# Another order of the group norm between the scan and the output projection, its low parts on GpSimd, and alternating PSUM banks at the end of the state space model

## The chip, the cores and the metric

The kernel runs on one core of one Trainium2 chip. The metric is the device time of one execution in microseconds, as the median over several executions. The profiled execution of the kernel before took 3902.99 us, of which its span (first to last instruction) is 3901.2 us.

## The reference, cut to what matters

The network works on 1024 positions of 1024 features, all in float32, and has three layers. The first layer is a gated linear recurrence, the second an RWKV-7 time mix, each followed by a feed-forward part, and the third a hybrid of a long convolution and a state space model. Two places of it matter here.

The end of the RWKV time mix is a group norm over each head of 64 features, a bias, a bonus term, a gate and the output projection:

```python
mean = jnp.mean(y, axis=-1, keepdims=True)
var = jnp.mean(jnp.square(y - mean), axis=-1, keepdims=True)
yn = ((y - mean) * lax.rsqrt(var + RW_GN_EPS)).reshape(B, T, D)
yn = yn * ln_w + ln_b
out = (yn + bonus) * g
return out @ w_o, v_first
```

The state space model of the third layer computes, for each of 32 groups of 16 channels, a complex linear recurrence of 64 states and reads it out; a GELU follows. Beside it stands the layer norm of the convolution's result:

```python
_, _, s_re, s_im = lax.associative_scan(combine, (a_re, a_im, bu_re, bu_im), axis=1)
y = (einsum("blgp,ghp->blgh", s_re, c_re) - einsum("blgp,ghp->blgh", s_im, c_im) + d * uf)
y = gelu(y)
cu = silu(layer_norm(cu, conv_ln_g, conv_ln_b))
```

## The kernel before, in words

Features lie on the 128 partitions in eight tiles (`DT` = 8) of 1024 positions each. Every engine has its own instruction list, written out by hand in the order in which it is issued; semaphores (`after(name, n)`, `tick(name)`) join the lists. An engine that meets a wait stands still with all that is behind it. PSUM is used as four banks of 128 x 1024 float32, which the profile calls psA to psD (`ps[0]` to `ps[3]`). Blocks end with a barrier between the engines.

**Projections.** A large matrix product is made of strips of weights (class `Flow`). Each operand is split into a high part (rounded to `float32r` by a ScalarE copy, `hi`, line 259) and a low part (the rest, one subtraction; for weights on GpSimd, `lo`, line 269), and three products are added: high x high, high x low, low x high. One tile k of one strip is six matmuls of 512 columns (`product`, line 302).

**The group norm, `TimeMixOut` (lines 3036 to 3232).** For each of the eight tiles k of `o` (rw_o in the profile): TensorE sums over the heads (`head_sum` in `sums`, line 3087), VectorE subtracts the mean (`centre`, line 3186), ScalarE squares (`square`, line 3124), TensorE sums the squares (`head_sum` in `spreads`), ScalarE takes Ln and then Exp with a scale of -0.5 (`roots`, lines 3131 and 3135), VectorE applies the root, the bias with the bonus and the gate in three instructions (`gated`, lines 3192, 3196 and 3199), ScalarE makes the high part (`high`, line 3139) and VectorE the low part (`low`, line 3203). Then TensorE multiplies tile k with the first two strips `at[0]` and `at[1]` of the output projection. When all eight tiles are through, it does the six strips `at[2:]` whole. SyncE loads the bonus tile (`load`) and brings one tile of H back (`back`) behind `gated`; `fast.load` then fetches the weights of the feed-forward part.

The order before goes in pairs q = 0 to 3. TensorE: sums 0 and 1, spreads 0, sums 2, spreads 1, sums 3, and then for each pair the products of its two tiles, with spreads 2 behind the products of pair 0 and spreads 3 behind those of pair 1. VectorE: six `centre`, then for each pair two `gated` and two `low`, with the last two `centre` behind pair 0. ScalarE: high parts of a pair, then the roots of the pair after the next. The banks of spreads 2 (psC, psD) are those of sums 3, so they need the last two `centre`; the buffers of the roots go round by four. GpSimd has only the low parts of weights in this stretch.

**The end of the state space model, `ssm` (lines 3775 to 4044).** The 32 groups go in four parts k (`SU` = 4). VectorE makes the states of part k (`group`, about a dozen instructions). TensorE's `outputs(k)` (lines 3861 and 3863) makes for each of eight groups one matmul of the direct part and two of the states, all into psD; VectorE copies the two halves of psD out (`outputs` on VectorE, line 3997); TensorE's `back(k)` turns them over into psA (line 3870), and ScalarE's GELU reads psA (line 3950). TensorE's `outputs(k)` waits until psD has been copied out (`sy_c` at 2k), and `back(k)` until the GELU before has read psA (`sy_t` at k). Between them lies the variance of the layer norm (`variance`, line 3885, psB), whose root ScalarE makes with Ln and Exp (lines 3946, 3948); VectorE's `normed` (line 4009) applies it to the eight tiles of H, four before its `outputs(2)` and four before its `outputs(3)`. At the barrier behind it the block of the next projections begins (first weights `w_glu`, line 248).

## Time and profile before

| | |
|---|---|
| median of 3 runs | 3901.69 us (3901.31 to 3909.06) |
| the profiled execution | 3902.99 us |
| its span | 3901.2 us |
| mean granted TensorE clock | 0.965 |
| busy: PE, PEld, DVE, ACT, POOL | 92%, 74%, 66%, 39%, 30% of the span |
| group norm with the first two strips | about 2027.9 to 2110.9 us of the span |
| state space model | about 3488.7 to 3602.4 us of the span |

In the rows PE is TensorE's matmuls, PEld its weight loads, DVE is VectorE, ACT ScalarE, POOL GpSimd and SP SyncE. A row of the timeline gives the start in us, the length in us, the engine, the line and operation, what it writes and reads with its shape, how often it stands there (xN, merged), and in brackets the idle time of the engine before it and what ended it.

### The profile page before, as it was taken

The page shows a single profiled execution, that of the slowest core. Times are in us where ns is not written, and L with a number is a line of the kernel's source. Part 1 is how long each engine was busy: PE and PEld are TensorE (multiplying, and loading weights), DVE is VectorE, ACT ScalarE, POOL GpSimd, SP SyncE. Part 2 cuts the span into 40 slices and gives each one's busy share as a digit, 9 for nine tenths or more (in the row PEclk, how much of TensorE's full clock was granted, in tenths as well). Part 3 has the DMA queues.
Part 4 walks back from the last instruction along what each step waited for, and adds up shares of the span by engine and source line. Part 5 has one row for each costly group of instructions (what it writes and reads, how often), then busy time and mean ns, then how long its engine had stood idle before and what let it go on. Part 6 is the DMA issues. An engine that isn't in the chain of part 4 may idle for free. (4 is left out here: it accounts for less than half of the span.)

```text
span 3901.2 us, 57647 instructions
## 1 busy us (share of the span) xinstructions
PE 3577.1 (92%) x24956; PEld 2905.9 (74%) x24956; DVE 2570.5 (66%) x2287; ACT 1536.5 (39%) x1634; POOL 1152.7 (30%) x521
## 2 busy tenths in 40 slices
PE   8999999999989998877777999999998999997997
PEld 6778788878767776666655788878886888875775
DVE  5554767687756857766655666678758888816532
ACT  5563432344534338744444433343443222113312
POOL 1125454555421211233322445445520000000211
PEclk9999999999999999999998999999999999997998
DMA  2112233344212245712113123253312222231322
GB/s 97 49 38 62 70 108 104 104 158 171 68 55 82 107 144 163 237 63 73 69 46 113 46 98 111 92 185 131 115 48 106 75 75 78 82 141 30 144 95 103
DMA packets 187037, 383.74 MB, mean 98 GB/s; under 512 B 16080, under 2 KB 84816, under 8 KB 181008
## 3 DMA queue, kind: packets, MB, share of 16 engines
q1 hardware_dynamic: 149216, 307.68, 23.8%
q10 hardware_dynamic: 37568, 72.36, 5.0%
q8 instruction: 198, 3.24, 0.3%
q14 instruction: 55, 0.45, 0.0%
HBM read 273.57 MB, written 105.91 MB: 97 GB/s over the span
## 5 line engine op out<-in xcount | busy, mean ns | idle before, releaser
L3817 POOL MEMSET ssm_toep<- 128x4096 f32 x1 | 3.5, 3512 | 545.7 <-POOLq L3516 545.7
L3403 DVE SCALAR_TENSOR_TENSOR H<-hy_cu,par,H 128x1024 f32<-128x1024 f32 x120 | 153.5, 1279 | 0.0
L269 POOL TENSOR_TENSOR wlo1C<-fast_raw,whi1C 128x1024 fp32r<-128x1024 f32 (+1 forms) x40 | 110.9, 2773 | 113.4 <-ACT whi1C L259 113.4
L269 POOL TENSOR_TENSOR wlo0B<-fast_raw,whi0B 128x1024 fp32r<-128x1024 f32 (+1 forms) x40 | 112.1, 2802 | 107.5 <-ACT whi0B L259 107.5
L3403 DVE SCALAR_TENSOR_TENSOR hy_odd<-hy_cu,par,hy_odd 128x1024 f32<-128x1024 f32 x112 | 143.3, 1280 | 0.0
L269 POOL TENSOR_TENSOR wlo1A<-fast_raw,whi1A 128x1024 fp32r<-128x1024 f32 (+1 forms) x40 | 111.4, 2785 | 105.6 <-ACT whi1A L259 105.6
L269 POOL TENSOR_TENSOR wlo1B<-fast_raw,whi1B 128x1024 fp32r<-128x1024 f32 (+1 forms) x39 | 107.9, 2766 | 114.3 <-ACT whi1B L259 114.3
L1007 DVE TENSOR_TENSOR fast_xl<-fast_xr,fast_xh 128x2048 fp32r<-128x2048 f32 (+1 forms) x42 | 127.5, 3059 | 21.3 <-ACT fast_xh L848 21.3
L269 POOL TENSOR_TENSOR wlo0A<-fast_raw,whi0A 128x1024 fp32r<-128x1024 f32 (+1 forms) x40 | 110.1, 2753 | 105.0 <-ACT whi0A L259 105.0
L269 POOL TENSOR_TENSOR wlo0C<-fast_raw,whi0C 128x1024 fp32r<-128x1024 f32 (+1 forms) x39 | 108.0, 2770 | 104.2 <-ACT whi0C L259 104.2
L942 DVE TENSOR_TENSOR fast_g<-fast_g,flow_rms 128x1024 f32<-128x1024 f32 x44 | 127.0, 2886 | 1.5
L2942 DVE STREAM_TRANSPOSE sc_XX<-sc_XX 64x512 f32<-64x512 f32 x160 | 112.9, 706 | 17.3 <-POOL sc_XX L2882 12.4
L2889 POOL TENSOR_TENSOR sc_NT<-sc_Gx,sc_level 128x512 f32<-128x512 f32 x80 | 100.1, 1282 | 78.1 <-PE psB L2627 43.4
L834 ACT ACTIVATE fast_g<-fast_g 128x1024 f32<-128x1024 f32 x44 | 46.6, 1060 | 127.4 <-DVE fast_g L942 127.4
L2627 PE MATMUL psA<-sc_XX,sc_NT 64*64 64x64 f32 x1280 | 55.7, 234 | 40.9 <-issue 40.8
L269 POOL TENSOR_TENSOR wlo0A<-wraw0A,whi0A 128x1024 fp32r<-128x1024 f32 (+2 forms) x15 | 33.8, 2256 | 195.5 <-ACT whi0A L259 195.5
L269 POOL TENSOR_TENSOR wlo0C<-wraw0A,whi0C 128x1024 fp32r<-128x1024 f32 (+1 forms) x16 | 37.6, 2347 | 172.7 <-ACT whi0C L259 172.7
L2627 PEld LDWEIGHTS psA<-sc_XX,sc_NT 64*64 64x64 f32 x1280 | 48.6, 143 | 47.1 <-issue 45.8
L2627 PE MATMUL psB<-sc_XX,sc_NT 64*64 64x64 f32 x1280 | 51.7, 235 | 31.6 <-issue 29.9
L848 ACT ACTIVATE fast_xh<-fast_xr 128x2048 fp32r<-128x2048 f32 (+1 forms) x42 | 74.1, 1765 | 12.1 <-DMA fast_xr<-ffn_x 11.8
L2363 DVE SCALAR_TENSOR_TENSOR flow_rms<-flow_rms,hawk_room_b 128x1024 f32<-128x1024 f32 x10 | 12.3, 1225 | 101.0 <-ACT flow_rms L2202 101.0
L959 DVE TENSOR_TENSOR fast_g<-fast_g,fast_s 128x1024 f32<-128x1024 f32 x22 | 72.7, 3303 | 0.8
(1458 smaller groups left out, 11925.8 us busy)
## 6 DMA issues: line engine op xcount, KB each, us to landing
fast_raw<-ffn_in_dram SPq DMA_DIRECT2D x88, 512.0 KB, 3.8
fast_xr<-ffn_x SPq DMA_DIRECT2D x28, 1024.0 KB, 6.1
sc_ops<-rw_arbkv SPq DMA_DIRECT2D x15, 1280.0 KB, 7.2
fast_raw<-ffn_out_dram SPq DMA_DIRECT2D x32, 512.0 KB, 3.8
wraw1A<-hybrid_in_dram SPq DMA_DIRECT2D x24, 512.0 KB, 3.4
wraw1B<-hybrid_in_dram SPq DMA_DIRECT2D x24, 512.0 KB, 3.3
ffn_x<-fast_g ACTq DMA_DIRECT2D x22, 512.0 KB, 3.3
ffn_x<-fast_e ACTq DMA_DIRECT2D x22, 512.0 KB, 2.8
```

The source lines that it names most:

```text
L269: eng.tensor_tensor(self.slot(wlo, n), self.raw[n], self.slot(whi, n).bitcast(fp32), ALU.subtract)\
L834: act.activation(g[:, :, z, :], g[:, :, z, :], ACT.Silu).then_inc(*tick("q_silu"))
L848: act.activation(part(hx, v, i), part(lr, v, i), ACT.Copy).then_inc(*tick("x7_hi"))
L942: dve.tensor_tensor(g[:, :, h, :], g[:, :, h, :], wide(h), ALU.mult).then_inc(*tick("q_g"))
L959: dve.tensor_tensor(g[:, :, 1, :], g[:, :, 1, :], s[:, :, :], ALU.mult).then_inc(*tick("q_h"))
L1007: dve.tensor_tensor(part(lx, v, i), part(lr, v, i), part(hx, v, i).bitcast(fp32), ALU.subtract)\
L2363: dve.scalar_tensor_tensor(out=e, in0=e, scalar=1.0, in1=tz, op0=ALU.add, op1=ALU.mult)\
L2627: mm = pe.matmul(eight[2 * a][half(e), m, :], NT[half(1 - e), a, (5 * (n // 2) + l) % 3, m, :], XX[half(1 - e), n % 4, 1, m, :], start=Tru ...
L2889: pl.tensor_tensor(NT[:, n % 2, k % 3, :, :], Gx[:, n % 2, :, :], by_m(slevel[:, l, :]), ALU.mult)\
L2942: dve.transpose(XX[half(1 - e), n % 4, 1, :, :].rearrange("p m t -> p (m t)"), XX[half(e), n % 4, 0, :, :].rearrange("p m t -> p (m t)")). ...
L3403: op = dve.scalar_tensor_tensor(out=acc, in0=c[:, j:j + T], scalar=w, in1=acc, op0=ALU.mult, op1=ALU.add)
L3817: pl.memset(toep[:, :, :], 0.0).then_inc(*tick("st_zero"))
```

## The change

It has two parts, which touch different stages.

In the group norm, TensorE's spreads 2 (tiles 4 and 5) now stand behind sums 3, ahead of every product, and spreads 3 behind the products of tile 1. VectorE does `gated(0)`, then the last two `centre`, then `gated(1)` to `gated(7)`; it has no `low` any more. The eight `low` stand on GpSimd, six of them ahead of the weight strip 2 (`W.lo(pl, 2)`) and two behind it. ScalarE's high parts are spread one by one between squares and roots, and the high part of the weight strip 2 stands ahead of the last two.

In the state space model, parts k write psD and psC in turn (`ps[3 - k % 2]`), so that `outputs(k)` waits for the copy of part k - 2 (part 1 for `sb_b`, the last reader of psC). TensorE's `outputs(3)` is cut in two halves of four groups with `back(2)` between them, and `back(3)` goes to psB (`ps[k // (SU - 1)]`), which it may once the Ln has read the variance (`ln_log`). VectorE does its `outputs(2)` before any `normed`, then six of them, `outputs(3)`, and the last two.

```diff
                     sums(2)
                     spreads(1)
                     sums(3)
-                    for q in range(DT // 2):
-                        if q == 0:
-                            W.begin(pe, at[0])
-                            W.begin(pe, at[1])
-                        for k in (2 * q, 2 * q + 1):
-                            pe.wait_ge(*after("ro_lo", k + 1))
-                            W.product(pe, at[0], k, *self.xs[k])
-                            W.product(pe, at[1], k, *self.xs[k])
-                        if q < 2:
-                            spreads(q + 2)
+                    spreads(2)
+                    W.begin(pe, at[0])
+                    W.begin(pe, at[1])
+                    for k in range(DT):
+                        pe.wait_ge(*after("ro_lo", k + 1))
+                        W.product(pe, at[0], k, *self.xs[k])
+                        W.product(pe, at[1], k, *self.xs[k])
+                        if k == 1:
+                            spreads(3)
...
                     squares(1)
                     roots(0)
                     squares(2)
+                    high(0)
                     roots(1)
-                    for q in range(DT // 2):
-                        high(2 * q)
-                        high(2 * q + 1)
-                        if q == 0:
-                            squares(3)
-                        if q + 2 < DT // 2:
-                            roots(q + 2)
+                    high(1)
+                    squares(3)
+                    high(2)
+                    roots(2)
+                    high(3)
+                    roots(3)
+                    high(4)
+                    high(5)
                     W.hi(act, 2)
+                    high(6)
+                    high(7)
...
                 @block.gpsimd
                 def _(pl):
+                    def low(k):
+                        pl.wait_ge(*after("ro_hi", k + 1))
+                        pl.tensor_tensor(self.lo[:, k, :], o[:, k, :], self.hi[:, k, :].bitcast(fp32), ALU.subtract).then_inc(*tick("ro_lo"))
+
+                    W.lo(pl, 1)
+                    for k in range(6):
+                        low(k)
+                    W.lo(pl, 2)
+                    for k in range(6, DT):
+                        low(k)
...
-                    for q in range(DT // 2):
-                        gated(2 * q)
-                        gated(2 * q + 1)
-                        low(2 * q)
-                        low(2 * q + 1)
-                        if q == 0:
-                            centre(DT - 2)
-                            centre(DT - 1)
+                    gated(0)
+                    centre(DT - 2)
+                    centre(DT - 1)
+                    for k in range(1, DT):
+                        gated(k)
...
-                        def outputs(k):
+                        def outputs(k, groups=range(8)):
...
+                            elif k == 1:
+                                pe.wait_ge(*after("sb_b", SU))
                             else:
-                                pe.wait_ge(*after("sy_c", 2 * k))
-                            for g in range(8):
+                                pe.wait_ge(*after("sy_c", 2 * k - 2))
+                            for g in groups:
                                 q, rows = g // 2, slice(64 * (g % 2), 64 * (g % 2) + 64)
-                                to = ps[3][:, g % 2, q * P:(q + 1) * P]
+                                to = ps[3 - k % 2][:, g % 2, q * P:(q + 1) * P]
...
                         def back(k):
                             pe.wait_ge(*after("sy_c", 2 * k + 2))
-                            pe.wait_ge(*after("su_c", SU) if k == 0 else after("sy_t", k))
+                            if k == 0:
+                                pe.wait_ge(*after("su_c", SU))
+                            elif k < SU - 1:
+                                pe.wait_ge(*after("sy_t", k))
+                            else:
+                                pe.wait_ge(*after("ln_log", 1))
...
-                        for k in range(SU + 1):
-                            if k < SU:
-                                outputs(k)
-                            if k > 0:
-                                back(k - 1)
-                            if k == 0:
-                                variance(0)
-                                variance(1)
-                            if k == 1:
-                                for m in range(2, DT):
-                                    variance(m)
+                        outputs(0)
+                        variance(0)
+                        variance(1)
+                        outputs(1)
+                        back(0)
+                        for m in range(2, DT):
+                            variance(m)
+                        outputs(2)
+                        back(1)
+                        outputs(3, range(4))
+                        back(2)
+                        outputs(3, range(4, 8))
+                        back(3)
...
                         group(3)
-                        for k in range(4):
-                            normed(k)
                         outputs(2)
-                        for k in range(4, DT):
+                        for k in range(6):
                             normed(k)
                         outputs(3)
+                        for k in range(6, DT):
+                            normed(k)
```

## Rows read from the trace of the kernel before

**Rows 1.** The page, busy time, share of the span and instructions of each engine.

```profile
PE 3577.1 (92%) x24956; PEld 2905.9 (74%) x24956; DVE 2570.5 (66%) x2287; ACT 1536.5 (39%) x1634; POOL 1152.7 (30%) x521
```

**Rows 2.** Windows: stretch, length, busy us (instructions) by engine, granted clock, DMA.

```profile
2027.90:2110.90 83.00, 56.57 (x160) 34.09 (x161) 50.26 (x43) 48.24 (x46) 7.17 (x3) 0.84 0.41 143
2110.90:2198.00 87.10, 86.65 (x379) 70.78 (x378) 48.49 (x38) 43.10 (x48) 41.63 (x22) 1.00 0.12 39
3488.70:3602.40 113.70, 93.27 (x480) 64.41 (x480) 76.18 (x90) 31.79 (x26) 3.51 (x1) 0.83 0.29 87
```

**Rows 3.** Timeline of TensorE in the group norm.

```profile
2047.38 1.88 PE L3087 MATMUL psD<-rw_o,const 128*128 128x512 f32 x4
2057.32 1.19 PE L302 MATMUL psA<-ro_oh,whi1A 128*128 128x512 f32 x2 [8.06 <-DVE ro_ol L3203]
2061.71 0.62 PE L302 MATMUL psA<-ro_oh,whi1A 128*128 128x512 f32 x2
...
2095.47 1.22 PE L302 MATMUL psA<-ro_oh,whi1A 128*128 128x512 f32 x2 [6.72 <-DVE ro_ol L3203]
2105.29 0.74 PE L302 MATMUL psA<-ro_oh,whi1A 128*128 128x512 f32 x2 [1.20 <-DVE ro_ol L3203]
2110.91 0.62 PE L302 MATMUL psC<-ro_oh,whi1C 128*128 128x512 f32 x2
```

**Rows 4.** Timeline of VectorE in the group norm.

```profile
2045.42 1.28 DVE L3192 SCALAR_TENSOR_TENSOR rw_o<-rw_o,par,flow_rms 128x1024 f32<-128x1024 f32 x1 [2.29 <-ACT flow_rms L3135]
...
2104.02 2.43 DVE L3203 TENSOR_TENSOR ro_ol<-rw_o,ro_oh 128x1024 fp32r<-128x1024 f32 x2
```

**Rows 5.** Timeline of ScalarE in the group norm: roots and high parts.

```profile
2050.55 1.11 ACT L3131 ACTIVATE ro_rs<-psB,eps 128x1024 f32<-128x1024 f32 x1
2051.68 1.28 ACT L3135 ACT_TABLE_LOAD   x1
2052.97 2.00 ACT L3135 ACTIVATE ro_rs<-ro_rs 128x1024 f32<-128x1024 f32 x2
2054.88 1.99 ACT L3139 ACTIVATE ro_oh<-rw_o 128x1024 fp32r<-128x1024 f32 x2
```

**Rows 6.** Timeline of GpSimd and VectorE, three places where both have work.

```profile
2034.94 2.37 POOL L269 TENSOR_TENSOR wlo1A<-wraw1A,whi1A 128x1024 fp32r<-128x1024 f32 x1 [48.85 <-ACT whi1A L259]
2035.04 1.23 DVE L3186 SCALAR_TENSOR_TENSOR rw_o<-psD,rw_o 128x1024 f32<-128x1024 f32 x1 [0.49 <-PE psD L3087]
...
2419.31 3.46 POOL L269 TENSOR_TENSOR wlo1B<-fast_raw,whi1B 128x1024 fp32r<-128x1024 f32 x1 [3.40 <-ACT whi1B L259]
...
3630.26 2.41 POOL L269 TENSOR_TENSOR wlo2B<-wraw2A,whi2B 128x1024 fp32r<-128x1024 f32 x1 [3.21 <-ACT whi2B L259]
3630.34 3.42 DVE L3711 TENSOR_TENSOR hb_cl<-H,hb_ch 128x1024 fp32r<-128x1024 f32 x1
```

**Rows 7.** Timeline of TensorE at the end of the state space model.

```profile
3575.45 1.09 PE L3870 MATMUL psA<-const,ssm_u 128*128 128x128 f32 x8
3579.45 0.64 PE L3861 MATMUL psD<-ssm_toep,ssm_ut 128*128 128x128 f32 x2 [2.91 <-DVE ssm_u L3997]
...
3594.29 1.97 PE L3870 MATMUL psA<-const,ssm_u 128*128 128x128 f32 x8
3598.44 1.94 PE L3870 MATMUL psA<-const,ssm_u 128*128 128x128 f32 x8 [2.18 <-ACT ssm_y L3950]
```

**Rows 8.** Timeline of VectorE and ScalarE there.

```profile
3573.24 4.87 DVE L4009 SCALAR_TENSOR_TENSOR H<-H,par,hb_rs 128x1024 f32<-128x1024 f32 x4 [3.37 <-ACT hb_rs L3948]
3578.03 1.28 DVE L3997 COPY ssm_u<-psD 128x512 f32<-128x512 f32 x2
...
3600.42 2.00 ACT L3950 ACTIVATE ssm_y<-psA 128x1024 f32<-128x1024 f32 x1 [2.12 <-PE psA L3870]
```

**Rows 9.** Windows at the end of the state space model.

```profile
3547.50:3556.80 9.30, 9.30 (x58) 7.35 (x57) 8.93 (x12) 1.06 (x1) 0.00 (x0) 1.00 0.00 0
3584.00:3590.00 6.00, 6.00 (x21) 4.66 (x22) 0.09 (x1) 0.00 (x0) 0.00 (x0) 0.50 0.00 0
```

More of the change, by code:

```diff
@@ L3199, in gated @@
                         dve.tensor_tensor(x, x, gates_kept[k], ALU.mult).then_inc(*tick("ro_gated"))
-                    def low(k):
-                        dve.wait_ge(*after("ro_hi", k + 1))
-                        dve.tensor_tensor(self.lo[:, k, :], o[:, k, :], self.hi[:, k, :].bitcast(fp32), ALU.subtract).then_inc(*tick("ro_lo"))
                     for k in range(6):
                         centre(k)
-                    for q in range(DT // 2):
-                        gated(2 * q)
-                        gated(2 * q + 1)
-                        low(2 * q)
-                        low(2 * q + 1)
-                        if q == 0:
-                            centre(DT - 2)
-                            centre(DT - 1)
+                    gated(0)
[3 more added lines that the diff above has]
+                        gated(k)
                     for m, n in enumerate(at):
@@ L3863, in outputs @@
                                     mm = pe.matmul(to, ee[rows, k, z, q, 0:SN], cq[rows, k, z, q, SSM_H:], start=False, stop=(z == 1))
-                            mm.then_inc(*tick("pe_yc"))
+                            if groups[-1] == 7:
+                                mm.then_inc(*tick("pe_yc"))
                         def back(k):
                             pe.wait_ge(*after("sy_c", 2 * k + 2))
-                            pe.wait_ge(*after("su_c", SU) if k == 0 else after("sy_t", k))
+                            if k == 0:
[4 more added lines that the diff above has]
+                                pe.wait_ge(*after("ln_log", 1))
                             for i in range(SC):
-                                mm = pe.transpose(ps[0][:, i // 4, (i % 4) * P:(i % 4 + 1) * P],
+                                mm = pe.transpose(ps[k // (SU - 1)][:, i // 4, (i % 4) * P:(i % 4 + 1) * P],
                                                   yc[:, k, i, :, :].rearrange("p g h -> p (g h)"), ident)
@@ L3949, in _ @@
                             act.wait_ge(*after("pe_yt", k + 1))
-                            act.activation(y[:, k, :].rearrange("p (c i) -> p i c", i=SC), flat[0].rearrange("p (i c) -> p i c", i=SC),
+                            act.activation(y[:, k, :].rearrange("p (c i) -> p i c", i=SC), flat[k // (SU - 1)].rearrange("p (i c) -> p i c", i=SC),
                                            ACT.Gelu_apprx_tanh).then_inc(*tick("sy_t"))
@@ L3997, in outputs @@
                                 dve.tensor_copy(yc[:, k, :, e:8:2, :].rearrange("p i q h -> p q i h"),
-                                                ps[3][:, e, :].rearrange("p (q i h) -> p q i h", q=4, i=SC)).then_inc(*tick("sy_c"))
+                                                ps[3 - k % 2][:, e, :].rearrange("p (q i h) -> p q i h", q=4, i=SC)).then_inc(*tick("sy_c"))
                         ch(dve.memset(ee[:, :, :, :, 0:1], 0.0))
```

## The prediction

> **What bounds the kernel now.** The busy shares of the profile's page come first: PE is busy 92% of the span, so time is to be had only where TensorE stands or runs at the low clock [rows 1]. The windows over the two changed stages show both: in the group norm TensorE is busy 56.6 of 83.0 us at a mean granted clock of 0.84, in the state space model 93.3 of 113.7 us at 0.83, while in the 87 us behind the group norm it is busy all but 0.5 us at 1.00 [rows 2]. So whatever the group norm finishes earlier is handed on: the strips behind it are TensorE's own work, back to back. No other engine is the bound of either stage as a whole (VectorE 50 and ScalarE 48 of 83 us), so each is a chain of hand-overs.
>
> In the group norm the reader sees TensorE end the spreads at 2049.26 (2047.38 + 1.88), stand 8.06 us for a low part, later 6.72 and 1.20 us (a like gap of 10.15 lies between), and begin strip 2 without a gap at 2110.91 [rows 3]. Behind each long gap the first pair of strips takes 4.4 us (2057.32 to 2061.71), where at full clock it takes 2.73. The chain through those gaps is spreads, roots, two `gated`, two high parts, two low parts, products, and only then the next spreads. VectorE ends `gated(7)` at 2104.02, where the last two low parts begin [rows 4].
>
> In the state space model `outputs(3)` starts 2.91 us after `back(1)`, because it waits for the copy of psD, and then takes from 3579.45 to 3594.29, 14.8 us [rows 7], at clock 0.50 [rows 9]. `outputs(1)` and `back(0)` together took 9.3 us at 1.00 [rows 9]. `back(2)` stands behind it, and `back(3)` waits 2.18 us for the GELU of part 2; the last GELU ends at 3602.42 [rows 8], and the next block starts there.
>
> **Part A, the group norm.** Nothing changes until `gated(0)` starts at 2045.42. The steps used below: one `gated` is three instructions of 1.28, 1.28 and 1.22, with hand-over 3.8 us [rows 4]; the same lengths stand in all eight. A pair's roots are a table load 1.28, two Ln 2.1, a table load 1.28, two Exp 2.0, together 6.6 us; a high part is 1.0 [rows 5]. A low part leaves VectorE, where a pair costs 2.43 [rows 4], and costs GpSimd 2.4 each, by the like subtraction for weights [rows 6].
>
> What decides the sum is whether the two engines work side by side. At 3630.26 GpSimd starts such a subtraction of 2.41 us, and VectorE's, begun 0.08 us later, lasts 3.42 in place of 1.22: it stood until 3632.67. At 2419.31 it is GpSimd's that lasts 3.46. But VectorE's `centre` at 2035.04, which reads PSUM and one SBUF tile, takes 1.23 beside GpSimd's 2.37 [rows 6]. All three instructions of `gated` read two SBUF tiles, so I count them as excluded by each low part, and `centre` as free. The Trainium skill, "SBUF — State Buffer", section Who interferes with whom, has this as a rule: a VectorE instruction with two SBUF inputs and a GpSimd instruction that reads SBUF block each other fully, and the one issued first wins. It speaks against the move of the low parts, and by it the sum comes out as mine and not as the second rival's.
>
> The schedule: `gated(0)` ends at 2049.3, the last two `centre` at 2051.2. Spreads 2 run from about 2050 to 2053.7, not from 2064. ScalarE makes high 0 at 2049.3 to 2050, roots 1 until 2056.5, high 1, squares 3, high 2 until 2063, roots 2 until 2069.6, high 3, roots 3 until 2077, and high 4 and 5 by 2079.3. VectorE from 2051.2 has seven `gated`, 7 x 3.8 = 26.5 us, interrupted by eight GpSimd instructions (low 0 to 5, weight strip 2, low 6); the first costs 1.1, the others about 2.2 each, 16.7 us in all. It waits hardly at all in between (about 1 us for roots 4, partly paid by an interruption already counted). So `gated(7)` ends at 2051.2 + 26.5 + 16.7 = 2094.4, against 2104.0. High 7 ends at 2095.5 and low 7 at 2098.0. The product of tile 6 has been done by 2096.5; that of tile 7 is 2.7 us at full clock and 5.1 at the low one. TensorE has stood 1.5 us before it and 3 to 5 us before tile 6, so I take 4.4 to 4.9, and strip 2 begins at 2102.4 to 2102.9. Its weights are split by 2087.4. That is 8.5 to 8.0 us before 2110.91; I take 8.0.
>
> What is moved past what: SyncE's bonus loads and H transfers wait for `gated` in the same order, with at least 7.6 us from each load's start to its use; the feed-forward weights start with `gated(7)`, 8 us before strip 2 instead of 6.9. Squares 3 and high 0 to 2 cost ScalarE nothing on the path, since VectorE is the later one. The added waits are GpSimd's for high parts: behind low 6 and 7 stands only later weight work, and in front of strip 2's low part low 5, which cannot hold TensorE before the last product. TensorE's early spreads 2 put products 0 and 1 behind 3.6 us that it would else have idled.
>
> Bounds of A: if nothing excludes, `gated(7)` waits for roots 3 only and ends near 2081, GpSimd ends its row of low parts at 2087.4, and the last products end at 2094.6: 16.3 us gained. If each of the eight interruptions costs VectorE a whole further turn (3.3 in place of 2.2, as a third party at each switch), 8.8 more are lost and A is worth about -0.5 to 0. I take 8.0, from the measured 3.42.
>
> **Part B, the state space model.** Up to `back(1)` (3575.45 to 3576.4) TensorE keeps its order without gaps, and `outputs(1)` could start no sooner before. Then `outputs(3)`, first half, starts at 3576.5: psC was copied out long before, and the states of part 3 are ready. At full clock a whole `outputs` is 9.3 - 0.95 = 8.4 us [rows 7, 9], a half 4.2: to 3580.7. VectorE now copies part 2 at 3575.5 to 3576.8, ahead of `normed`, and the GELU of part 1 ends at 3578.6 as before, so `back(2)` runs without a wait, to 3581.7. Second half to 3585.9. Six `normed` of 1.2 [rows 8] end at 3584.0, so VectorE copies at 3585.9 to 3587.2; `back(3)` needs only the Ln, to 3588.3; the last GELU, 2.0, ends at 3590.3, and the last two `normed` at 3589.6. Against 3602.42 that is 12.1 us; I take 12.0. What hid the four `normed` was GELU and copy; six of them have 9 us of matmuls over them.
>
> Of the 12 us, 6.5 are the clock: 14.8 - 8.4. It fell while TensorE stood for 2.91 us, and that gap is gone. But 15 us of unbroken `outputs` did not bring it back, so this kind of work is near the point where the clock isn't kept, and now 18.8 us of it stand in a row. The lower bound: the clock falls at 3579.5 all the same. Then the first half ends at 3581.6, `back(2)` at 3583.5, the second half, 7.4, at 3590.9, copy, `back(3)` and GELU (1.3 + 1.9 + 2.0) at 3596.3: 6.1 gained. Low from 3576.5 on: 3.7. No bound lies above 12.5.
>
> The Trainium skill, "TensorE: Matmul & The Clock Gate", section What's actually happening, says that sustained activity releases the throttle. Rows 9 don't agree for this work: busy all of the time, and 0.50. By that rule of the Trainium skill B would be 12.0 whatever the gap; by the row it hangs on never losing the clock.
>
> **Sum.** 3902.99 - 8.0 - 12.0 = 3883.0 for an execution like the profiled one. The median of the runs is 1.3 lower, so 3881.7.
>
> **The rivals.** *The clock falls in B anyway*: for it, no `outputs` run longer than 9.3 us at 1.00 is in the trace and none at 0.50 recovers; against it, the clock held through three such runs and fell only after a gap. 3.7 to 6.1 in place of 12.0: 3887.6 to 3890.0. The Trainium skill, "TensorE: Matmul & The Clock Gate", section Part 4: PE-mode transpose, says that transposes don't count as activity for the clock; by it `back(1)` and `back(2)` inside the long run would make this rival likelier.
>
> *GpSimd and VectorE don't exclude each other here*: for it, only two-input subtractions and additions are seen blocked in rows 6, not `gated` itself; against it, these differ in nothing that should matter. A is 16.3: 3873.4.
>
> *Exclusion at a full turn each*: A is worth nothing, 3889.7. Speaking for it is only that so many hand-overs in a row stand nowhere in the trace.
>
> *Only one part arrives*, because a transfer or the block behind fills its place: for B, the next block's first matmul waits for weights loaded after the barrier, which move with it; for A rows 2 show no slack. If neither arrived, 3901.7.
>
> *Slower*: the products of tiles 6 and 7 start at the low clock after a chain of short stands, and the clock stays low in the strips behind, as it stayed in `outputs(3)`. A strip is 10.9 us at full clock and 20.5 at the low one (0.857 against 0.455 per pair of matmuls behind 2095.47), 9.6 lost for each. After two strips at the low clock the 20 us are gone, after three the kernel is slower, 3910. Against it: behind all three long gaps these matmuls had the full clock within 3.4 to 6.1 us.
>
> **How the numbers follow.** Forecast 0.66, with its own range 3877 to 3887; clock lost in B 0.12; no exclusion 0.08; full turns 0.06; one part or none arrives 0.05; slower 0.03. The range leaves out the no-exclusion case and what lies above 3891: 3876 to 3891. A measurement of this kernel tells about 0.2%, 7.8 us, from no change. Faster by more than that (below 3893.9) are the first four cases, 0.92, less a little for both small gains together: 0.91. Within it 0.06, slower 0.03.
>
> **What would show it.** A right: no `low` on VectorE, `gated` instructions of 3.4 us in about eight places, between the second `centre` pair and strip 2; strip 2 starts 75 us (2102.7 - 2027.9) into the stage in place of 83. Wrong if `gated` keeps 1.28 throughout. B right: `outputs(3)` begins directly behind `back(1)` at clock 1.00 and the stage is 101.7 us long in place of 113.7; wrong if the clock reads 0.50 before `back(3)`. The handing on is wrong if TensorE shows new gaps in the strips behind.

## The result, and the profile after

The changed kernel takes 3883.6 us (median of 6 runs, 3874.46 to 3891.65) against 3901.5 us (median of 6, 3899.82 to 3909.06). The ratio is 0.9949, 95% interval 0.9933 to 0.9965: 20 us faster by the ratio, 14 to 26 by its interval. The forecast was 3881.7 us, 20 us faster. The profiled execution took 3877.22 us, one of the two fastest, with a span of 3875.4 us, 25.8 shorter than that of the profiled execution before.

Windows over the two stages and the strips behind the group norm, the changed kernel; they answer to [rows 2]. Columns as there.

```profile
2028.60:2101.90 73.30, 58.07 (x160) 34.23 (x161) 56.58 (x35) 48.28 (x46) 29.07 (x11) 0.88 0.46 161
2101.90:2189.00 87.10, 86.65 (x379) 70.81 (x378) 48.32 (x38) 43.07 (x48) 41.65 (x22) 1.00 0.12 40
3476.20:3578.10 101.90, 85.17 (x480) 58.56 (x480) 76.19 (x90) 31.88 (x26) 3.43 (x1) 0.90 0.32 97
```

The group norm is 73.3 us long in place of 83.0, the state space model 101.9 in place of 113.7. The strips behind the group norm have the same 86.65 busy us in 87.10: what was gained was handed on. The 25.8 us of the span add up from the stretches between the same instructions of both traces: group norm -9.7, state space model -11.8, from strip 2 to the start of the state space model -3.6 (1377.8 to 1374.2), before the group norm +0.7, behind the state space model -1.4. The last three, 4.3 us, lie where nothing was edited. Most of the -3.6 arises at one place of the feed-forward part, about 520 us behind strip 2, where the kernel before stands 2.31 us and goes on at the low clock, while the changed kernel has neither there. TensorE of the kernel before there:

```profile
2633.99 0.66 PE L491 MATMUL psD<-fast_xh,whi1C 128*128 128x512 f32 x1 [2.31 <-DVE fast_xl L1007]
```

Whether this is an effect of the change stays open. The six traces with low parts on GpSimd (the changed kernel and five of those below) have 1373.4 to 1374.3 us in this stretch, the two with the old group norm 1377.9. But of three later kernels with one and the same third order of the group norm (low parts on VectorE, the high part of weight strip 2 early), two show 1377.7 and one 1374.6, so a difference of this size also comes without any edit.

Timeline of TensorE in the group norm, changed kernel, answering to [rows 3]:

```profile
2051.30 1.95 PE L3087 MATMUL psC<-ple_gate,const 128*128 128x512 f32 x4 [1.30 <-DVE rw_o L3199]
...
2061.98 1.22 PE L302 MATMUL psA<-ro_oh,whi1A 128*128 128x512 f32 x2 [4.21 <-POOL ro_ol L3179]
...
2093.21 1.22 PE L302 MATMUL psA<-ro_oh,whi1A 128*128 128x512 f32 x2 [4.07 <-POOL ro_ol L3179]
2099.08 0.73 PE L302 MATMUL psA<-ro_oh,whi1A 128*128 128x512 f32 x2 [0.38 <-POOL ro_ol L3179]
2101.92 0.62 PE L302 MATMUL psC<-ro_oh,whi1C 128*128 128x512 f32 x2
```

The reader sees spreads 2 at 2051.3, ahead of all products, and in place of stands of 8.06, 10.15 and 6.72 us three of 4.07 to 4.21 us (two are shown) and short ones. The releaser is now GpSimd's low part. The last product, from 2099.08 to 2101.92, had the full clock; the one of tile 6, from 2093.21 on, the low clock for all of its 5.5 us.

Timelines of VectorE and then of GpSimd, changed kernel, at the end of the group norm; they answer to [rows 4] and [rows 6]:

```profile
2078.41 1.22 DVE L3212 TENSOR_TENSOR rw_o<-rw_o,tm_g_last 128x1024 f32<-128x1024 f32 x1
2079.55 3.45 DVE L3205 SCALAR_TENSOR_TENSOR rw_o<-rw_o,par,ro_rs 128x1024 f32<-128x1024 f32 x1
2083.04 3.27 DVE L3209 SCALAR_TENSOR_TENSOR rw_o<-ro_bn,par,rw_o 128x1024 f32<-128x1024 f32 x1
2086.34 3.30 DVE L3212 TENSOR_TENSOR rw_o<-rw_o,tm_g_last 128x1024 f32<-128x1024 f32 x1
2089.57 1.27 DVE L3205 SCALAR_TENSOR_TENSOR rw_o<-rw_o,par,ro_rs 128x1024 f32<-128x1024 f32 x1
2090.88 3.36 DVE L3209 SCALAR_TENSOR_TENSOR rw_o<-ro_bn,par,rw_o 128x1024 f32<-128x1024 f32 x1
2094.27 1.23 DVE L3212 TENSOR_TENSOR rw_o<-rw_o,tm_g_last 128x1024 f32<-128x1024 f32 x1
```

```profile
2079.57 5.66 POOL L3179 TENSOR_TENSOR ro_ol<-rw_o,ro_oh 128x1024 fp32r<-128x1024 f32 x2 [4.80 <-ACT ro_oh L3138]
2085.19 3.38 POOL L269 TENSOR_TENSOR wlo1C<-wraw1A,whi1C 128x1024 fp32r<-128x1024 f32 x1
2090.81 2.34 POOL L3179 TENSOR_TENSOR ro_ol<-rw_o,ro_oh 128x1024 fp32r<-128x1024 f32 x1 [2.25 <-ACT ro_oh L3138]
2096.66 2.36 POOL L3179 TENSOR_TENSOR ro_ol<-rw_o,ro_oh 128x1024 fp32r<-128x1024 f32 x1 [3.51 <-ACT ro_oh L3138]
```

`gated(6)` takes three instructions of 3.3 to 3.45 us, since GpSimd has three subtractions to do at that time (low 4, low 5 and weight strip 2), and the two engines take turns. In the whole stage eight of VectorE's `gated` instructions are lengthened, as many as GpSimd has subtractions ahead of the end of `gated(7)`. Together they are 15.7 us longer than they would be alone.

TensorE, VectorE and ScalarE at the end of the state space model, changed kernel; the rows answer to [rows 7, 8]:

```profile
3562.48 1.09 PE L3884 MATMUL psA<-const,ssm_u 128*128 128x128 f32 x8
3563.41 0.39 PE L3869 MATMUL psC<-ssm_toep,ssm_ut 128*128 128x128 f32 x2
3563.73 0.71 PE L3871 MATMUL psC<-ssm_cq,ssm_e 64*128 64x128 f32 x4
...
3574.04 1.97 PE L3884 MATMUL psB<-const,ssm_u 128*128 128x128 f32 x8 [1.38 <-DVE ssm_u L4013]
```

```profile
3562.65 1.29 DVE L4013 COPY ssm_u<-psD 128x512 f32<-128x512 f32 x2 [5.75 <-PE psD L3871]
3563.86 7.25 DVE L4025 SCALAR_TENSOR_TENSOR H<-H,par,hb_rs 128x1024 f32<-128x1024 f32 x6
3572.70 1.29 DVE L4013 COPY ssm_u<-psC 128x512 f32<-128x512 f32 x2 [1.58 <-PE psC L3871]
```

```profile
3568.66 2.06 ACT L3966 ACTIVATE ssm_y<-psA 128x1024 f32<-128x1024 f32 x1 [3.00 <-PE psA L3884]
3576.05 2.00 ACT L3966 ACTIVATE ssm_y<-psB 128x1024 f32<-128x1024 f32 x1 [5.32 <-PE psB L3884]
```

`outputs(3)` begins directly behind `back(1)`, at 3563.41, and is over at 3572.65: 9.2 us with `back(2)` in it, where it took 14.8 alone. The windows over the row from `outputs(2)` to the end of `outputs(3)`, over `outputs(3)` with `back(2)` alone, and over `back(3)`, show the clock:

```profile
3554.10:3572.60 18.50, 18.50 (x113) 14.59 (x111) 11.16 (x12) 11.40 (x8) 0.00 (x0) 1.00 0.00 0
3563.40:3572.60 9.20, 9.20 (x58) 7.25 (x56) 7.71 (x7) 4.12 (x2) 0.00 (x0) 1.00 0.00 0
3574.00:3576.00 2.00, 1.96 (x8) 1.57 (x8) 2.00 (x2) 0.00 (x0) 0.00 (x0) 0.50 0.00 0
```

### The profile page after: what moved, and what is told of

It is laid out like the page before. It is cut to its first block and busy times, and to the rows that moved or that the text cites. A ratio compares the mean times of both kernels' runs of the same rounds, so it can differ in the third digit from the quotient of the medians.

```text
span 3875.4 us, 57648 instructions
## 1 busy us (share of the span) xinstructions
PE 3568.7 (92%) x24956; PEld 2898.7 (75%) x24956; DVE 2576.1 (66%) x2279; ACT 1536.1 (40%) x1634; POOL 1176.7 (30%) x529
## 5 line engine op out<-in xcount | busy, mean ns | idle before, releaser
L269 POOL TENSOR_TENSOR wlo0A<-fast_raw,whi0A 128x1024 fp32r<-128x1024 f32 (+1 forms) x40 | 110.1, 2752 | 105.1 <-ACT whi0A L259 105.1
L2882 POOL TENSOR_TENSOR sc_XX<-sc_XX,sc_eye 128x512 f32<-128x512 f32 x16 | 20.3, 1268 | 179.7 <-DVE sc_XX L2937 179.7
```

Source lines behind the costliest of these rows:

```text
L269: eng.tensor_tensor(self.slot(wlo, n), self.raw[n], self.slot(whi, n).bitcast(fp32), ALU.subtract)\
L2882: pl.tensor_tensor(XX[:, n % 4, 0, :, :], XX[:, n % 4, 0, :, :], by_m(seye[:, :]), ALU.add)\
```

## The experiments

The theory after the result: each part does by itself what its stage shows; GpSimd's low parts cost VectorE more than they take off it; the clock in the state space model is lost in a stand or just behind it, and `outputs` doesn't win it back. Rivals are named with each kernel. Stage lengths below are counted alike in each trace: the group norm from its first head sum to strip 2, the state space model from its first mean to the end of the last GELU. The ratios are to the kernel before on the same chip. The reader should weigh them with two facts: the times of one and the same code differ by 17 us between executions of the changed kernel and by up to 21 us in the kernels below, and each trace shows one execution.

**Each part alone.** The first kernel has the changed group norm only, the second the changed state space model only; their edits are those of the diff above.

> Part A alone: the group norm as changed, the state space model as before. My theory (the two parts are independent and what the group norm gains is handed on): strip 2 starts 9.7 us earlier than before, counted from the start of the stage (74.0 in place of 83.0 us or a little less), and the kernel is 8 to 10 us faster, ratio 0.9975 +- 0.0005. The rival (much of the 18 to 26 us comes from elsewhere, by chance between runs): under 5 us.

> Part B alone: the end of the state space model as changed, the group norm as before. My theory: the last GELU ends 11.4 us earlier against the start of the stage, clock 1.00 in all of outputs(3), and the kernel is 11 to 12 us faster, ratio 0.9970 +- 0.0005. The rival that the clock is lost in some executions of this stage: a few times stand 6 to 8 us above the others, and the gain is 4 to 8 us in those.

Norm alone: 3892.22 us (7 runs, 3887.63 to 3899.81), ratio 0.9971, interval 0.9960 to 0.9981; group norm 73.32 us, state space model 113.36. State space model alone: 3891.32 us (5 runs, 3889.37 to 3893.42), ratio 0.9966, interval 0.9952 to 0.9979; group norm 83.07, state space model 102.26. Both did in their stage what they do together, to within 0.4 us. By the ratios they are worth 11.3 and 13.3 us, so the rival of the first (under 5 us, the rest chance) fell. The sum is 24.6, against 20 for both; the intervals (the sum's reaches from 16 to 34) allow that they simply add. That the clock is lost in some executions of the second didn't show in its five times.

**Low parts on VectorE again.** The order of the changed kernel stays, the eight low parts move:

```diff
 # VectorE
                     gated(0)
                     centre(DT - 2)
                     centre(DT - 1)
-                    for k in range(1, DT):
+                    low(0)
+                    gated(1)
+                    for k in range(2, DT):
                         gated(k)
+                        low(k - 1)
+                    low(DT - 1)
 # GpSimd: without low
```

> As the changed kernel, but the eight low parts of the group norm are on VectorE again, each one gated part later (gated 2, low 1, gated 3, low 2 and so on). My theory (the two engines exclude each other, so each low part on GpSimd costs VectorE 2.2 us where it would itself need 1.2): gated(7) ends some 7 us earlier than in the changed kernel, strip 2 starts 6 to 9 us earlier, total 6 to 9 us faster than the changed kernel, ratio to before about 0.993. The rival (GpSimd takes the low parts off VectorE's hands and that is what gains): VectorE has 9.8 us more to do, strip 2 starts 3 to 9 us later than in the changed kernel.

3872.73 us (4 runs, 3870.55 to 3874.38), ratio 0.9918, interval 0.9905 to 0.9932. The group norm is 68.21 us long, 5.1 less than in the changed kernel. Timeline of VectorE in that kernel, `gated(6)` to the last low parts:

```profile
2078.30 1.28 DVE L3195 SCALAR_TENSOR_TENSOR rw_o<-rw_o,par,ro_rs 128x1024 f32<-128x1024 f32 x1
2079.62 3.29 DVE L3199 SCALAR_TENSOR_TENSOR rw_o<-ro_bn,par,rw_o 128x1024 f32<-128x1024 f32 x1
2082.95 1.23 DVE L3202 TENSOR_TENSOR rw_o<-rw_o,tm_g_last 128x1024 f32<-128x1024 f32 x1
2084.09 1.22 DVE L3206 TENSOR_TENSOR ro_ol<-rw_o,ro_oh 128x1024 fp32r<-128x1024 f32 x1
...
2089.00 2.43 DVE L3206 TENSOR_TENSOR ro_ol<-rw_o,ro_oh 128x1024 fp32r<-128x1024 f32 x2
```

Only one `gated` is still lengthened, 3.29 us, by the one GpSimd subtraction that is left there (weight strip 2). VectorE is through with `gated(7)` at about 2089.0, 60.7 us into the stage, against 66.9 in the changed kernel, although six low parts of its own, 7.3 us, stand ahead of that; the last two follow. The rival (GpSimd takes work off VectorE) has fallen: the new order alone gives 14.8 us, and the move to GpSimd takes 5.1 back, which leaves the 9.7 that the group norm gained. Which share the order of each of the three engines has in the 14.8, no run separates. The 5.1 are a little less than the 6 to 9 expected: `gated(7)` came 6.1 us earlier, but TensorE, whose product of tile 5 ran at the low clock (5.3 us), had those of tiles 6 and 7 still to do. The whole kernel became 12 us faster by the two ratios, more than the stage explains; their intervals only just don't touch.

**The weight's low part last.**

```diff
 # GpSimd
                     W.lo(pl, 1)
-                    for k in range(6):
-                        low(k)
-                    W.lo(pl, 2)
-                    for k in range(6, DT):
+                    for k in range(DT):
                         low(k)
```

> As the changed kernel, but GpSimd's low part of weight strip 2 stands behind all eight low parts of the group norm instead of between the sixth and the seventh. One interruption fewer ahead of gated(7): by my theory gated(7), the last low part and strip 2 come 2.0 to 2.3 us earlier, the weight's low part then ends about when the last product does. Rival (GpSimd's own row of low parts decides, not the exclusion): the same 2.2 us, but gated(7) on VectorE ends where it did.

3884.1 us (5 runs, 3878.52 to 3885.55), ratio 0.9945, interval 0.9932 to 0.9957, not to be told from the changed kernel. The group norm is 71.25 us long, 2.05 less, and `gated(7)` ends 2.06 us earlier in it, so the rival, by which it would end where it did, fell: one interruption of VectorE is worth what was said. The same trace brought something else: its state space model is 110.1 us long, 8 more, with the same code there. Windows over states(3), `outputs(0)`, the two variances and `outputs(1)` of that kernel:

```profile
3514.50:3518.00 3.50, 3.50 (x32) 3.23 (x32) 3.36 (x5) 0.00 (x0) 0.00 (x0) 0.50 0.00 0
3518.00:3533.00 15.00, 15.00 (x50) 11.40 (x48) 6.61 (x9) 1.02 (x1) 0.00 (x0) 0.50 0.01 1
3533.00:3538.70 5.70, 5.70 (x9) 2.42 (x9) 5.28 (x9) 1.06 (x1) 0.00 (x0) 0.61 0.00 0
3538.80:3547.00 8.20, 8.20 (x49) 6.37 (x47) 7.00 (x9) 1.06 (x1) 0.00 (x0) 1.00 0.00 0
```

TensorE is busy all of the time, yet the clock stays at 1.2 GHz through all 15 us of `outputs(0)` and rises only in the variances, whose matmuls have 512 columns. In the kernel before and in the changed one the clock had risen in the last 0.3 to 0.4 us of states(3) (mean 0.54 and 0.56), just before `outputs(0)`.

**Variances ahead of outputs(0).**

```diff
+                        variance(0)
+                        variance(1)
                         outputs(0)
-                        variance(0)
-                        variance(1)
                         outputs(1)
```

> As the changed kernel, but TensorE's variance of tiles 0 and 1 (wide matmuls, 512 columns) stands ahead of outputs(0) instead of behind it. One trace has shown outputs(0) at clock 0.50 from end to end where the matmuls before it did not raise the clock in time, and that stage 8 us longer. My theory (the clock of this stage is a lottery that outputs can't win back once lost, and it is behind most of the spread of the times): the two wide products raise the clock before outputs(0) in every execution, the stage is 99 to 101 us long, the spread of the times shrinks and the median falls 1 to 4 us under the changed kernel's. Rival (the spread comes from elsewhere, the scan above all): same median within 1 us and same spread.

3879.87 us (5 runs, 3870.86 to 3882.12), ratio 0.9938, interval 0.9925 to 0.9951. In the trace states(3) again ended at the low clock (3.68 us), the variances raised it, and the stage was 101.8 us long: in one execution the edit did what it was meant to. That it does so in each is not shown. The median fell by 3.7 us, as expected, but the two intervals overlap, and five times that still spread over 11 us, against six over 17, don't bear out that this stage makes most of the spread. The group norm of this trace, the same code as in the changed kernel, took 76.4 us against 73.3. Its first head sums ran at the low clock, which cost 1.7 us, and its last product stood 2.84 us and then took 4.45 us in place of 2.84. Window over that product:

```profile
2103.34:2107.79 4.45, 4.45 (x13) 3.49 (x13) 1.22 (x1) 1.43 (x2) 0.43 (x1) 0.62 1.03 371
```

**One bank.**

```diff
-                            elif k == 1:
-                                pe.wait_ge(*after("sb_b", SU))
                             else:
-                                pe.wait_ge(*after("sy_c", 2 * k - 2))
+                                pe.wait_ge(*after("sy_c", 2 * k))
...
-                                to = ps[3 - k % 2][:, g % 2, q * P:(q + 1) * P]
+                                to = ps[3][:, g % 2, q * P:(q + 1) * P]
... # and VectorE's copy reads ps[3] for every k
```

> As the changed kernel, but all four outputs(k) go to psD and wait for its copy as before; the earlier copy on VectorE, the split outputs(3) and back(3) in psB stay. My theory (what made the gap before outputs(3), and with it the low clock, was VectorE's four normed ahead of the copy, not the one bank): the gap is 0.4 to 0.5 us, the clock stays at 1.00, and the stage is only 0.5 us longer than in the changed kernel, 100.5 us. Rival (the alternating bank is what pays): outputs(3) starts 1.5 us or more late, the clock is lost, the stage is 106 us or longer.

3888.06 us (6 runs, 3869.81 to 3891.2), ratio 0.9955, interval 0.9939 to 0.9972. The stage is 111.0 us long in the trace, a length that the rival had named (106 or more), but not for the rival's reason: `outputs(0)` had the low clock from end to end, as above, which costs 8 us by itself. The place in question, TensorE of that kernel in front of `outputs(3)` and the window over it:

```profile
3574.56 0.46 PE L3867 MATMUL psD<-ssm_toep,ssm_ut 128*128 128x128 f32 x2 [0.51 <-DVE ssm_u L4011]
```

```profile
3574.60:3583.80 9.20, 9.20 (x56) 7.28 (x56) 6.98 (x6) 3.60 (x2) 0.00 (x0) 1.00 0.00 0
```

The stand is 0.51 us, the clock stays at 1.00, and from there to the end of the last GELU it is 14.7 us as in the changed kernel (14.6). Against the kernel with the same loss in `outputs(0)` (110.1) the stage is 0.9 longer. So it was VectorE's four `normed` ahead of the copy that made the stand of 2.91 us, and the alternating banks give about 0.5 to 0.9 us of the 11.8. Counted from the rows, the stand and the clock of `outputs(3)` are together 9.7 us, the second bank's share in it; about 1.8 lie behind `outputs(3)`, where its split and `back(3)` in psB act, which no run tests by themselves, and 0.4 ahead of `back(1)`, where the order of TensorE is unchanged.

**A stand put back.**

```diff
                         back(1)
+                        pe.wait_ge(*after("ln_n", 3))
                         outputs(3, range(4))
```

> As the changed kernel, with one wait more: TensorE waits for the third normed before outputs(3), which puts a gap of about 4 us there. My theory (the clock falls in the gap and outputs can't raise it again): outputs(3) runs at 0.50, and the stage is 4 + 6.5 = 10 to 11 us longer than in the changed kernel. Rival (the clock was lost for another reason, or comes back within outputs(3)): 4 to 6 us longer.

3893.24 us (12 runs, 3883.98 to 3899.74), ratio 0.9973, interval 0.9963 to 0.9983. The stage is 113.2 us long, 11.3 more than in the changed kernel. Timeline and windows of that kernel, the stand and `outputs(3)` with `back(2)` behind it:

```profile
3571.54 0.80 PE L3869 MATMUL psC<-ssm_toep,ssm_ut 128*128 128x128 f32 x2 [4.01 <-DVE H L4026]
```

```profile
3567.50:3571.50 4.00, 0.03 (x1) 0.00 (x0) 4.00 (x5) 2.04 (x1) 0.00 (x0) 0.86 0.00 0
3571.50:3588.20 16.70, 16.66 (x56) 13.00 (x56) 3.57 (x3) 2.01 (x1) 0.00 (x0) 0.50 0.00 0
```

4.0 us of stand, and 16.7 us in place of 9.2 behind it, all at 0.50. By the rival (the clock comes back within `outputs(3)`) it would have been 4 to 6 us in all. So this is the price of the clock in this stage shown by itself: 7.5 us on top of a stand of 4.0.

**Versions to beat both.** Three kernels have the low parts on VectorE and the high part of weight strip 2 ahead of `high(0)`:

```diff
                     squares(2)
+                    W.hi(act, 2)
                     high(0)
...
                     high(5)
-                    W.hi(act, 2)
                     high(6)
```

The first also rearranges the state space model: variances 0 to 5 in TensorE's idle time before states(3), `outputs(0)` before states(3), variances 6 and 7 behind `back(0)` and `back(1)`, the root behind the second GELU, ScalarE's squares 0 to 5 ahead of its own last work on the states, and four `normed` in place of six ahead of VectorE's last copy. The second moves variance 5 behind states(3). The third has the changed kernel's order with variances 0 and 1 ahead.

```diff
 # TensorE, first; the second has range(5), and variance(5) behind states(SU - 1)
-                        states(SU - 1)
+                        for m in range(6):
+                            variance(m)
                         pe.wait_ge(*after("ln_c", DT))
                         outputs(0)
-                        variance(0)
-                        variance(1)
+                        states(SU - 1)
                         outputs(1)
                         back(0)
-                        for m in range(2, DT):
-                            variance(m)
+                        variance(6)
                         outputs(2)
                         back(1)
+                        variance(7)
                         outputs(3, range(4))
```

> A version that may beat both. Group norm with the low parts on VectorE and the high part of weight strip 2 ahead of high(0), where ScalarE waits anyway, so that GpSimd's subtraction doesn't stand among the gated; state space model with variances 0 to 5 in TensorE's idle time before states(3), outputs(0) before states(3), variance 6 behind back(0), variance 7 behind back(1), the root behind the second GELU and four normed before the last copy. My theory: strip 2 starts 2 us earlier than with low parts on VectorE alone (66 us into the stage), and the state space model is 92 us long at best (VectorE's four groups end 1.3 us earlier, then outputs(3) at full clock), in all 8 to 11 us under the 3872.7 of that version: 3862 to 3865. Rival: a short gap before outputs(2) or outputs(3) loses the clock and 6 us of it.

> As the version with both stages rearranged, but variance 5 stands behind states(3), in the 1.78 us in which TensorE stood there and after which outputs(1) lost the clock. My theory (a short stand followed by outputs loses the clock; wide matmuls in it keep it): outputs(1) stays at 1.00, VectorE's copy comes 3 us earlier, the state space model takes 96 to 97 us in place of 99.5, median 2 to 4 us lower than that version's. Rival (each gap of 1 to 2 us that is left can lose the clock just as well): no gain, the loss moves to another outputs.

> The group norm of that version (low parts on VectorE, high part of weight strip 2 early) with the changed kernel's state space model, variances 0 and 1 ahead of outputs(0). My theory: group norm 65.5 us, state space model 101.8 us, so 2 to 3 us slower than the version with both stages rearranged and 6 to 8 us faster than the one that has only the variances ahead: about 3871 to 3874. Rival (the parts take from each other): above 3877.

First: 3870.54 us (4 runs, 3868.07 to 3874.45), ratio 0.9919 (0.9906 to 0.9932); group norm 65.5, state space model 99.5. Second: 3873.4 us (5 runs, 3865.87 to 3874.23), 0.9919 (0.9906 to 0.9931); 67.2 and 101.0. Third: 3870.4 us (5 runs, 3870.19 to 3875.6), 0.9919 (0.9906 to 0.9933); 65.5 and 102.3. The early high part did its 2 us and a bit in the stage (68.2 to 65.5); that it shows in the kernel's time can't be said. The 92 us hoped for in the state space model of the first and the 96 to 97 of the second didn't come: the first lost the clock in `outputs(1)`, within 1.9 us of its start behind a stand of 1.78, the second in `outputs(3)`, within 1.4 us of its start behind one of 1.61. So both medians missed their forecast, 3862 to 3865 us and 2 to 4 us under the first. Windows of the first and then of the second kernel:

```profile
3529.00:3530.90 1.90, 1.90 (x10) 1.54 (x11) 1.80 (x5) 1.88 (x3) 0.00 (x0) 0.92 0.00 0
3531.00:3544.40 13.40, 13.40 (x47) 10.49 (x47) 10.74 (x15) 1.04 (x1) 0.00 (x0) 0.50 0.00 0
```

```profile
3552.60:3554.00 1.40, 1.40 (x7) 1.09 (x8) 1.26 (x2) 1.37 (x3) 0.00 (x0) 0.83 0.02 6
3554.00:3569.00 15.00, 14.50 (x50) 11.28 (x49) 5.34 (x5) 5.42 (x4) 0.00 (x0) 0.50 0.00 0
```

My rival for the second kernel was right: the loss moved to another `outputs`. The third met its forecast for both stages (65.5 and 101.8 us), but its median equals that of the first, where 2 to 3 us more were said. All four kernels with the low parts on VectorE are within each other's intervals, 32 us under the kernel before and, by the ratios, 12 under the changed one; which of them is best these runs can't tell.

## Why the prediction was right, point by point

*The sum.* 3902.99 - 8.0 - 12.0: measured 9.7 and 11.8 in the traces, and 20 by the ratio. The two profiled executions differ by 25.8, of which 4.3 lie outside both stages; the forecast was made for the median, 3881.7, and 3883.6 was measured. That the mechanism and the two stages came out is no luck; that the median fits to 2 us is in part luck, since the six times reach from 3874 to 3892.

*A, the schedule.* `gated(7)` was put at 2094.4; in the changed trace it ends at 2095.5, which is 2094.8 when 0.7 us is taken off for the later start of the stage. The low part of tile 7 was put at 2098.0: 2099.02 less 0.7 is 2098.3. Eight lengthened `gated` instructions were said, and there are eight, of 2.42 to 3.45 us. Two small errors cancel in it: the interruptions came to 15.7 us in place of 16.7 (and 1.1 with seven of 2.2 would have been 16.5), and VectorE stood 1.04 us for the roots of tiles 4 and 5, which was put at next to nothing. Spreads 2 came at 2051.3, 2050.6 less the 0.7, and cost nothing where they stand.

*A, the term that was mis-sized.* The last product was taken at 4.4 to 4.9 us, at a partly low clock. In this trace it took 2.84 at full clock. The product of tile 6, said to be done by 2096.5, ran at the low clock throughout and ended at 2098.7, so TensorE stood only 0.38 us in place of 1.5 and had the full clock again. That is the 1.7 us between 8.0 and 9.7. But five traces of this same group norm show 73.3, 73.3, 74.6, 76.4 and 76.4 us. In the last three the product of tile 6 had the full clock, TensorE then stood 2.8 us, and the last product took 4.45 us, as the sum had it; the two of 76.4 lost 1.7 more in the first head sums. These three come from one chip, and the second of the two 73.3 from another; whether the chip or the draw decides is not shown. The mean of the five is 74.8, so 8.0 was near what it gives on the whole.

*The exclusion.* The rival without it (A 16.3) and the rival with a full turn for each interruption (A 0) were both refuted by the rows, and moving the low parts back showed what the exclusion costs: 5.1 us. The prediction had the cost in its sum, 16.7 us of interruptions, of which the weight's subtraction is about 2.2, but I didn't set beside the other 14.5 that the same low parts cost VectorE 9.7 us. Read so, the move was a loss of 4.8 us on paper already. The Trainium skill, "SBUF — State Buffer", section Who interferes with whom, has the rule by which both follow, and these traces agree with it: seven instructions of 1.22 to 1.28 us take 3.26 to 3.45, and the eighth, begun 1.0 us after GpSimd's, 2.42.

*B.* Gap gone, clock kept, stage 101.9 us where 101.7 was said. The last GELU came later than the sum had it since `back(3)` ran at the low clock, 1.97 in place of 1.1 us, after a stand of 1.38; half of that was made good ahead of `back(1)`. One reading of the kernel before was wrong: the clock did not fall while TensorE stood for 2.91 us. Window over that stand:

```profile
3576.50:3579.40 2.90, 0.04 (x1) 0.00 (x0) 2.90 (x5) 2.04 (x1) 0.00 (x0) 1.00 0.00 0
```

It fell as `outputs(3)` began (0.66 over its first 0.45 us). The sum doesn't depend on which, since both go when the stand goes. The share of the banks is small as well: they are in the change's name, but the copy ahead of `normed` does it, and two banks add under 1 us.

*The rival that the clock is lost in B anyway* was given 0.12 for one reason and is true for another. Where nothing was put into the long row from `outputs(2)` to the end of `outputs(3)`, as in the changed kernel, it was never lost there in the profiled executions (six of six), with the transposes of `back(1)` and `back(2)` in the row. But it can be missing from the start, in `outputs(0)`: two of the eight traces with the first half of this stage as before show that, 8 us each. The kernel before has the same first half, so this widens both and favours neither; its times reach from 3893.7 to 3909.1, and no trace of one of its slower executions was taken. The Trainium skill, "TensorE: Matmul & The Clock Gate", section What's actually happening, has sustained activity release the throttle. These runs contradict it for this work: 15 us busy without a break at 1.2 GHz in `outputs(0)` and 16.7 us in `outputs(3)`.

## What to carry to other kernels

Work moved from VectorE to GpSimd is not simply off VectorE's hands. Beside `centre`, which reads PSUM and one SBUF tile, it cost nothing here (1.23 us beside GpSimd's 2.37); beside `gated`, whose instructions have two SBUF inputs, it cost 2.0 to 2.2 us for 1.2 saved. When a stand of TensorE is followed by a stretch like `outputs`, count the clock, not the stand: 4.0 us of stand cost 11.3. An in-order engine that has both a copy on which TensorE waits and other work ready should do the copy first; that exchange was most of one part's gain, about 9 us of 11.8 counted from the rows, and the second bank under 1.

## What the runs showed of the hardware

`outputs` (128 columns, two of three matmuls over 64 rows) is busy 100% of its time at either level of the clock. It held 2.4 GHz for 18.5 us where it started there with no stand in front of it. In seven traces an `outputs` stood at 1.2 GHz (the kernel before and the one with the norm alone, and those with the weight's low part last, one bank, a stand put back and both rearranged stages), and in none did the clock rise in it, over 13 to 17 us each. In the variances behind it, matmuls of 512 columns over 128 rows, the clock was back 3.2 to 4.5 us after their start, and 2.4 us after it where they came behind states(3). Why it rose there and not in `outputs` stays open.

The clock was lost behind stands of only 1.6 and 1.8 us in front of `outputs`, and in or behind the stand of 1.38 us in front of `back(3)` in most traces. The products of the group norm kept it over most stands of 0.3 to 2.2 us, and lost it behind four of 1.86 to 2.00.

One and the same code in one stage took 73.3 to 76.4 us (five traces of the group norm) or 101.9 to 110.1 us (four of the state space model), largely by where the clock stood. A single trace of a kernel with many short stands is one draw.
